# Attention by key-stationary products: split values stationary, split transposed probabilities of two tiles moving, gates transposed instead of results, and a new order of the work around branch C

## What is computed

```python
pr = split_projection(x @ w_in)
o_a = dsa_attention(aq, ak, av, iq, ik, pr['i_w'])      # top-k sparse
o_b = moba_attention(bq, bk, ...)                        # block sparse
o_c = rms_norm(diff_attention(cq, ck, cv, lam), diff_norm) * (1.0 - lam_init)
o_d = mla_attention(qn, qr, kn, kr, dv)
o_e = memory_attention(...)
y = o * jax.nn.silu(z)                                   # z: gates, per branch
u = jnp.einsum('btnc,ncd->btnd', y, w_branch)
out = jnp.sum(jax.nn.sigmoid(g) * u, axis=2) @ w_out
return layer_norm(DN_ALPHA * x + out, ln_g, ln_b)
```

## Time and profile before

| | |
|---|---|
| median of 3 runs | 1382.11 us (1380.39 to 1382.39) |
| the profiled execution | 1384.15 us, of which the span is 1382.5 us |
| PE busy | 1328.0 us, 96% of the span |
| DVE, ACT, POOL busy | 661.8, 653.3, 669.9 us |
| mean granted TensorE clock | 0.985 |
| DMA | 116.47 MB, mean 84 GB/s |

### The profile page before, as it was taken

One profiled execution on the slowest core, in us unless ns is written; L12 is line 12 of the kernel. 1 busy time (PEld: TensorE's weight loads), 2 busy tenths in 40 slices (PEclk: granted clock), 3 DMA queues, 4 the chain that ended last, 5 costly groups with the idle time before them and its releaser, 6 DMA issues.

```text
span 1382.5 us, 19021 instructions
## 1 busy us (share of the span) xinstructions
PE 1328.0 (96%) x6872; PEld 1130.7 (82%) x6872; DVE 661.8 (48%) x1609; ACT 653.3 (47%) x1296; POOL 669.9 (48%) x850
## 2 busy tenths in 40 slices
PE   6999999999988999999999999999999899999995
PEld 5888878888877898888888888888888779888884
DVE  4646696433155753213265668753322665432044
ACT  4455345454275664423245543555434665643232
POOL 3543453255563444467464435334446434645764
PEclk9899999999998999999999999999999999999998
DMA  7322242231331143232413223223123213323221
GB/s 258 114 77 62 81 114 58 67 88 47 103 95 37 37 123 107 58 107 77 140 49 106 68 71 106 81 58 85 53 74 111 59 33 86 95 65 100 84 77 61
DMA packets 147052, 116.47 MB, mean 84 GB/s; under 512 B 5520, under 2 KB 131856, under 8 KB 146704
## 3 DMA queue, kind: packets, MB, share of 16 engines
q1 hardware_dynamic: 146816, 114.22, 27.8%
q10 hardware_dynamic: 144, 1.05, 0.2%
HBM read 112.10 MB, written 3.15 MB: 83 GB/s over the span
## 4 chain that ended last, share of the span: by engine, by line
PE 79%; DVE 12%; ACT 4%; issue 2%; POOL 1%; DMA 1%; SPq 0%; POOLq 0%; DVEq 0%; ACTq 0%
PE product L737 19%; PE product L738 18%; PE product L739 18%; PE context L977 5%; PE scores L949 3%; PE transposed L962 3%; PE branch_product L737 2%; PE branch_product L739 2%; PE branch_product L738 2%; DVE index_scores L1389 2%; DVE top_eight L1395 1%; DMA residual<-in_x_dram 1%; ACT score_operands L1001 1%; POOL residual L677 1%; DVE vector_scratch L1214 1%
## 5 line engine op out<-in xcount | busy, mean ns | idle before, releaser
L721 POOL TENSOR_TENSOR weights_rest<-raw_weights,weights_head 128x320 fp32r<-128x320 f32 (+3 forms) x672 | 540.1, 836 | 376.8 <-ACT weights_head L1001 376.8
L737 PE MATMUL product<-weights_head,stationary_head 128*128 128x512 f32 (+3 forms) x768 | 291.4, 379 | 7.8 <-POOL weights_rest L721 7.6
L1001 ACT ACTIVATE weights_head<-raw_weights 128x1280 fp32r<-128x1280 f32 (+4 forms) x178 | 198.3, 1115 | 200.3 <-PE product L739 153.5
L739 PE MATMUL product<-weights_head,stationary_rest 128*128 128x512 f32 (+3 forms) x768 | 285.6, 372 | 0.0
L738 PE MATMUL product<-weights_rest,stationary_head 128*128 128x512 f32 (+3 forms) x768 | 285.4, 372 | 0.0
L737 PE MATMUL product<-stationary_head,weights_head 128*128 128x512 f32 x640 | 263.5, 412 | 0.0
L738 PE MATMUL product<-stationary_rest,weights_head 128*128 128x512 f32 x640 | 252.6, 395 | 0.0
L739 PE MATMUL product<-stationary_head,weights_rest 128*128 128x512 f32 x640 | 252.1, 394 | 0.0
L704 POOL TENSOR_TENSOR merged<-merged,activated 128x256 f32<-128x256 f32 x128 | 93.0, 748 | 291.4 <-DVE activated L1533 291.2
L737 PEld LDWEIGHTS product<-weights_head,stationary_head 128*128 128x128 f32 x768 | 145.7, 190 | 29.8 <-POOL weights_rest L721 8.4
L739 PEld LDWEIGHTS product<-weights_head,stationary_rest 128*128 128x128 f32 x768 | 145.4, 189 | 23.7
(11 more groups left out here) (200 smaller groups left out, 1812.5 us busy)
## 6 DMA issues: line engine op xcount, KB each, us to landing
raw_weights<-in_w_in_dram SPq DMA_DIRECT2D x104, 512.0 KB, 3.7
raw_weights<-in_w_in_dram SPq DMA_DIRECT2D x72, 256.0 KB, 2.9
raw_weights<-in_w_branch_dram SPq DMA_DIRECT2D x80, 128.0 KB, 3.7
raw_weights<-in_w_out_dram SPq DMA_DIRECT2D x16, 512.0 KB, 3.6
merged<-in_w_mem_kv_dram SPq DMA_DIRECT2D x8, 512.0 KB, 7.3
raw_weights<-in_w_in_dram SPq DMA_DIRECT2D x8, 416.0 KB, 3.1
raw_weights<-in_w_in_dram SPq DMA_DIRECT2D x8, 296.0 KB, 3.8
residual<-in_x_dram SPq DMA_DIRECT2D x4, 512.0 KB, 11.4
```

Of the source, the lines that this page charges most:

```text
L721: ins = nc.gpsimd.tensor_tensor(WL[:, sw, part], RAW[:, sr, part], WH[:, sw, part].bitcast(F32), ALU.subtract)
L737: nc.tensor.matmul(dst, sh, mh, start=start, stop=False)
L739: return nc.tensor.matmul(dst, sl, mh, start=False, stop=stop)
L1001: return nc.scalar.activation(dst, src, ACT.Copy, scale=scale)
```

## The change

In branches A and D (WIDE):

- V is done once for two query tiles. Stationary are 128 keys of [values head, values rest] (`vs`, 128 columns); moving are the transposed probabilities of the tile pair, split in head `ph` and rest `pl`: 256 columns, or 128 where only the later tile sees the keys. All passes are fp32r. The output is the transposed result in two halves of 64 partitions, head and rest.
- The new step pr (DVE) makes `pl`; T's copy by ACT makes `ph`. The bank TP is free for the next T after pr, not after the copy. The new step vs splits a head's values (ACT, then DVE).
- fo is now an ACT copy of one half of the result (64 x 512), and the new step fa (DVE) adds the other half. fin multiplies the gate by the reciprocal row sums. The new step zj transposes the gates on PE into G2 and G3, where DVE multiplies them with the result; yj has no transpose left, and splits what lies in `probabilities_T` and `vector_scratch`.

For branch C, W stands half a step earlier and the pieces of ev and er are laid singly and earlier; the first qt uses the banks U and O, and the attention starts in chunk C1 instead of gA0. In chunk IX the groups go through three units for the first two tiles, in O1 through the units of a tile before the next tile, and l1 and l2 are spread among them. The early split of the next layer's first unit is gone, two splits stand earlier in `start`, and the fourth tile of x is loaded after two units of weights. The diff, cut:

```diff
+WIDE = "AD"
...
+def wide_steps(b):
...
+    if b == "D":
+        out = [[("qt", b, 0)], [("ev", b, 0)], [("er", b, 0), ("qt", b, 1)], [("ev", b, 1)], [("er", b, 1)], [("vs", b, 0)]]
+    else:
+        out = [[("qt", b, 0)], [("ev", b, 0), ("er", b, 0)], [("ev", b, 1), ("er", b, 1)], [("vs", b, 0)]]
+    for i in range(UNITS + LAG_V + 1):
+        first, second = [], []
+        u = i - LAG_V
+        if 0 <= u < UNITS and u % 2 == 1:
+            first.append(("V", b, u))
+        if u >= NT and u % NT == 0:
+            first.append(("fa", b, u // NT - 1))
+        if 0 <= i - LAG_T < UNITS:
+            first.append(("T", b, i - LAG_T))
+            second.append(("pr", b, i - LAG_T))
+        if i < UNITS:
+            second.append(("S", b, i))
+        if i in (4, 8):
+            second += prep_steps(b, 1 + i // 4)
+        if i in (5, 9):
+            first.append(("er", b, 1 + i // 4))
+        if 0 <= u < UNITS and u % NT == NT - 1:
+            j = u // NT
+            second += [("fo", b, j)] + ([("vs", b, j + 1)] if j + 1 < NH else []) + [("fin", b, j)]
+        if i == 12:
+            second.append(("zj", b, 0))
+        if u == UNITS:
+            second.append(("zj", b, 1))
+        out += [first, second]
+    return out
...
-    out = [[("qt", "C", 0)], [("ev", "C", 0, 0)], [("er", "C", 0, 0), ("ev", "C", 0, 1)], [("er", "C", 0, 1)], []]
...
+    out = [[("qt", "C", 0)]] + [[] for _ in range(5)]
+    early = {}
+    for j in range(NH):
+        for n in range(4):
+            m, part = divmod(n, 2)
+            at = {0: n - 5, 1: n}.get(j, 2 * (4 * j - 3) + 1 + n)
+            early.setdefault(at, []).append(("ev", "C", j, m, part))
+            early.setdefault(at + 1, []).insert(0, ("er", "C", j, m, part))
...
     for i in range(UNITS + 3):
-        first, second, third = [], [], []
+        first, second = [], []
         if 0 <= i - 3 < UNITS:
             first.append(("V", "C", i - 3))
+            if (i - 3) % NT == NT - 1:
+                first.append(("fo", "C", (i - 3) // NT))
+                second.append(("fin", "C", (i - 3) // NT))
         if 0 <= i - 2 < UNITS:
             first.append(("T", "C", i - 2))
         if i < UNITS:
             first.append(("S", "C", 2 * i))
-            second.append(("S", "C", 2 * i + 1))
+            second.insert(0, ("S", "C", 2 * i + 1))
         if 0 <= i - 1 < UNITS:
-            second.insert(0, ("W", i - 1))
-        second += late
-        late = []
-        if i >= 3 and (i - 3) % NT == NT - 1:
-            first.insert(1, ("fo", "C", (i - 3) // NT))
-            third.append(("fin", "C", (i - 3) // NT))
+            first.append(("W", i - 1))
         if i == 4:
-            third.append(("qt", "C", 1))
-        j, m = divmod(i + 3, 4)
-        if j < NH and m < 2 and i < UNITS:
-            third.append(("ev", "C", j, m))
-            late = [("er", "C", j, m)]
-        out += [first, second + third]
+            second.append(("qt", "C", 1))
+        out += [first + early.get(2 * i, []), second + early.get(2 * i + 1, [])]
...
-    ("lambda", ("gB1", 3, 3), ("C0", 0, 2), 0.0),
-    ("C attention", ("gA0", 0, 0), ("D0", 3, 2), 0.0),
+    ("lambda", ("gB0", 2, 0), ("gB0", 2, 0), 0.0),
+    ("C attention", ("C1", 0, 2), ("D0", 3, 1), 0.0),
...
+        order = [(u, t) for u in range(units(c)) for t in range(parts(c))]
+        if c == "IX":
+            order = [(u, t) for t in range(2) for u in range(3)] + [(u, t) for u in range(3) for t in (2, 3)] + [(3, t) for t in range(NT)]
+        elif c == "O1":
+            order = [(0, t) for t in range(NT)] + [(1, 0), (1, 1), (2, 0), (3, 0), (2, 1), (3, 1)] + [(u, t) for t in (2, 3) for u in range(1, 4)]
+        groups += [(c, u, t) for u, t in order]
...
-    start = [("ln0", 0), ("ln0", 1), ("mkv", 0), ("ln0", 2), ("xj", 0, 0), ("xj", 0, 1), ("ln0", 3), splits[0], ("mkv", 1),
-             ("xj", 1, 0), ("xj", 1, 1), ("ln0", 4), splits[1], splits[2]]
-    extra[at[(ORDER[0], 1, 0)]] += [("xj", 2, 0), ("xj", 2, 1)]
-    extra[at[(ORDER[0], 1, 1)]] += [("xj", 3, 0), ("xj", 3, 1)]
-    extra[at[(ORDER[0], 2, 0)]].append(("ek",))
+    start = [("ln0", 0), ("ln0", 1), ("mkv", 0), ("ln0", 2), ("xj", 0, 0), ("xj", 0, 1), splits[0], splits[1], ("mkv", 1),
+             ("xj", 1, 0), ("xj", 1, 1), ("ln0", 3), splits[2], ("ln0", 4)]
+    extra[at[(ORDER[0], 1, 1)]] += [("xj", 2, 0), ("xj", 2, 1)]
+    extra[at[(ORDER[0], 2, 1)]] += [("xj", 3, 0), ("xj", 3, 1)]
+    extra[at[(ORDER[0], 3, 1)]].append(("ek",))
...
-    extra[at[("O1", 2, 1)]] += [("ahead",) + WEIGHTS[0]]
-    extra[at[("O1", 3, 1)]] += [("l1", 0)]
-    extra[at[("O1", 3, 2)]] += [("l1", 1), ("l2", 0)]
-    extra[at[("O1", 3, 3)]] += [("l1", 2), ("l2", 1), ("l1", 3), ("l2", 2), ("l2", 3)]
+    for t in range(NT - 1):
+        i, j = {0: (("O1", 2, 1), ("O1", 3, 1))}.get(t, (("O1", 1, t + 1), ("O1", 2, t + 1)))
+        extra[at[i]].append(("l1", t))
+        extra[at[j]].append(("l2", t))
+    extra[at[("O1", 3, 3)]] += [("l1", 3), ("l2", 3)]
...
             if b == "C":
-                return G[2], G[3], HD * (j % 2)
+                (_, qs), (_, ks) = qt_banks(b, j // 2)
+                return qs, ks, HD * (j % 2)
...
+            if b == "D":
+                ph, pl = KLZ[:].rearrange("p a n -> p (a n)"), PL[:]
+            else:
+                ph, pl = (TL[:, a:a + 2, :].rearrange("p a n -> p (a n)") for a in (4, 6))
+            return [x.rearrange("p (i n) -> p i n", i=NT) for x in (ph, pl)] + [TL[:, 8, :].rearrange("p (i c d) -> p i c d", i=NT, c=2)]
...
+        def y_rows(k):
+            return PT if k == 0 else DS
...
-            load_x(3)
...
                 for i, item in enumerate(LOADS):
+                    if L == 0 and i == 2:
+                        load_x(3)
...
+                    elif kind == "zj":
+                        _, b, k = step
+                        claim(f"G{2 + k}")
+                        pe.wait_ge(final.sem, final.at(L, (b, 2 * k + 1)))
+                        for t in range(NT):
+                            last = nc.tensor.transpose(G[2 + k][:, t * P:(t + 1) * P],
+                                                       VZ[:, vz(b), t, BW + k * P:BW + (k + 1) * P], ident)
+                        last.then_inc(t_done.sem, t_done.step(step))
+                        freed[f"G{2 + k}"] = (gated, L, step)
...
+                        freed["TP"] = (rest, L, ("pr", b, u)) if b in WIDE else (moved, L, step)
+                    elif kind == "V" and step[1] in WIDE:
+                        _, b, u = step
+                        j, t = divmod(u, NT)
+                        ph, pl, vs = wide(b)
+                        if t == 1:
+                            claim("O")
+                            pe.wait_ge(rest.sem, rest.at(L, ("vs", b, j)))
+                        pe.wait_ge(rest.sem, rest.at(L, ("pr", b, u)))
+                        blocks = [(0, ph), (t, ph), (t, pl)] + [(i, p) for i in range(1, t) for p in (ph, pl)]
+                        blocks.insert(3 if t == 1 else 1, (0, pl))
+                        for n, (i, p) in enumerate(blocks):
+                            at = P if i == t else 0
+                            last = nc.tensor.matmul(O[:, (t - 1) * P + at:(t + 1) * P], vs[:, i].rearrange("p c d -> p (c d)"),
+                                                    p[:, i, at:2 * P], start=n == 0, stop=n == len(blocks) - 1)
+                        last.then_inc(v_done.sem, v_done.step((b, u)))
+                        if t == NT - 1:
+                            freed["O"] = (summed, L, (b, j))
...
+                    elif kind == "vs":
...
+                        _, b, j = step
+                        if j > 0:
+                            act.wait_ge(v_done.sem, v_done.at(L, (b, NT * j - 1)))
+                        else:
+                            act.wait_ge(copied.sem, copied.at(L, ("dk" if b == "D" else b + "1", NT - 1)))
+                        copy(wide(b)[2][:, :, j % 2, :], VZ[:, vz(b), :, j * HD:(j + 1) * HD]).then_inc(moved.sem, moved.step(step))
+                    elif kind == "fo" and step[1] in WIDE:
+                        _, b, j = step
+                        r, o = rows(j)
+                        act.wait_ge(v_done.sem, v_done.at(L, (b, NT * j + NT - 1)))
+                        copy(y_rows(j // 2)[r, :], O[o, :]).then_inc(moved.sem, moved.step(step))
...
+                        if b in WIDE:
+                            half = slice(t % 2 * P, (t % 2 + 1) * P)
+                            copy(wide(b)[0][:, 0:t + 1, half], TP[:, 0:w].rearrange("p (i n) -> p i n", n=P)).then_inc(moved.sem, moved.step(step))
...
+                    elif kind == "pr":
+                        _, b, u = step
+                        t, _, w = unit(b, u)
+                        ph, pl, _ = wide(b)
+                        half = slice(t % 2 * P, (t % 2 + 1) * P)
+                        dve.wait_ge(moved.sem, moved.at(L, ("T", b, u)))
```

(16 more changed lines are left out.)

129 lines of the change are left out of this document (76 added, 53 removed).

## The result

The changed kernel takes 1400.77 us (median of 4 runs, 1398.52 to 1401.18), the kernel before beside it 1381.25 us (4 runs, 1379.29 to 1382.39): ratio 1.014, 95% interval 1.0122 to 1.0157. It is **slower by 19.5 us**; 1355.8 us was predicted, with 1372 as the upper end. The span of its profiled execution is 1399.3 us against 1382.5.

What follows compares the result with a forecast made beforehand. PE was taken to bound the kernel, busy 1328.0 of 1382.5 us. Terms 1 to 5, -10.8 - 22 + 13 - 1 - 5.5 = -26.3 us, gave a median of 1355.8 us (chance 0.50), range 1340 to 1372.

Steps and rivals of the forecast that it cites:

- Term 4: Starts of the layers: first groups' 4.1 us wait goes, a like one comes at the third; -1 us, bounds -7 and +4.
- Term 3: Ends of heads in A and D: V waits for pr in DVE's queue; +13 us, bounds 0 and 26.
- Term 1: V in A and D: fewer, wider passes, 1.33 us a head instead of 2.0; -10.8 us, bounds -7 and -15.
- Term 2: Branch C: waits for W and er go, and their clock loss; -22 us, bounds -12 and -25.
- W's half: Branch C: W a half step earlier, two half steps ahead of T instead of one, fits with 2 us to spare.
- late next would be ACT: Branch C: sixteen copies for the first two heads fall in chunk C1 beside ACT's own activations; 3 us left for it.
- Rival B: Branch C keeps half of its waits, ACT or DVE being late: 12 us gained instead of 22, 1365.8 us; chance 0.12.
- Term 5: The tail: POOL has one tile left, 4 pieces, and the last transfers go earlier; -5.5 us, bounds -3 and -8.
- D: Rival: slower, 12 ends of heads wait 2 us each with a 2 us clock fall behind each; 1390.8 us; chance 0.04.
- rival C: Ends of heads: the SBUF port shared by DVE and POOL stretches vs and fin by 8 us; 1363.8 us; chance 0.08.

Runs made afterwards that it cites:

- e1: The changed kernel with the memory keys' split (ek) put back ahead of the fourth group of chunk IX: 1388.89 us, 11.9 us less than the changed kernel.
- e10: The changed kernel with the third weights' split of IX earlier and the load of tile 3 of x behind those weights' load: 1393.97 us, 6.8 us less.
- e2: The changed kernel with the whole start of a layer (IX's group order, ek, x loads, early split) as in the kernel before: 1380.03 us, 20.7 us less.
- e3: The changed kernel with the wide form off, A and D in the form before: 1388.28 us, 12.5 us less.
- e4: The changed kernel with branch C's plan, banks and eviction as in the kernel before: 1410.82 us, 10.0 us more; it doesn't compute the whole program.
- e7: The changed kernel with C's evictions (ev and er) of heads 2 and 3 one half step earlier: 1392.42 us, 8.4 us less.
- e5: e2 and e3 together, so that of the change only C and the tail are left: 1367.73 us, ratio 0.9911 to the kernel before.
- e8: e5 with e7's edit: 1363.99 us, ratio 0.9877 to the kernel before, 3.7 us below e5.
- e9: e8 with the wide form of A and D put back and their heads' closing step (reciprocals, fin) one tile later: 1365.21 us, ratio 0.9879 to before.
- e11: The changed kernel with the edits of e1, e7 and e10, and the heads' closing step in A and D one tile later: 1362.24 us, ratio 0.9850 to before.
- e12: e11 with branch A alone in the form before: 1361.29 us, ratio 0.9849 to the kernel before.

## Why the prediction was wrong

**Term 4, starts of the layers: -1 predicted, +18.6 measured, and the step that turned the sign.** Two things failed. The first is an omission: the working of the term has ln0, xj and the splits, and not ek, which the diff moves from behind (IX,2,0) to behind (IX,3,1). No one asked who waits for it (bank U, wanted by the index transposes) and what it is moved past on its engine (two tiles of index rotations). e1 shows 11.9 us for that alone. The second is "I find PE waiting there about as long": 4.1 us were carried over from a wait with another queue behind it, and it was 8.9. The prediction saw that the third split stood behind ln0 of the last tile, and then took the old wait's size instead of adding up the queue on ACT and POOL. e10 gives 6.8 us. Together 18.7 of the 20.7 us that e2 takes off.

**Term 3, waits at the ends of heads: +13 predicted, 16.4 measured.** The mechanism and the places were right: the three of A were given as 1.3, 2.0 and 0.5 and were 1.11, 2.08 and 1.16; those of D as 1.1, 0.4 and 1.1 and were 0.87, 0.43 and 1.13. Two kinds were left out: the last V of D (0.80) and small ones on V inside a head (0.27 to 0.37). And the clock: two falls in A cost 1.6 us each (A costs 5.5 us a layer with them, 3.9 in e2's trace, where there are none).

**Term 1, V: -10.8 predicted.** A head's V takes 1.52 us in the mean (1.56 in A, 1.48 in D), not 1.33, so the saving is 0.49 us a head, 7.8 us. The pitch of 0.12 was right inside a run of passes; the passes around them, at the start of a step and at each change of width, take more: the term is mis-sized, within its bound of -7. V, waits and falls give -7.8 + 16.4 + 3.2 = 11.8 us, beside 12.5 by e3 and 14.6 in the table. The rest stood in no term: in e2's trace the product passes of A and D, the same in number, take 1.0 us a layer more than before, and the transposes of D's keys 0.4.

**Term 2, C: -22 predicted, -11.3 measured** (10.0 by e4). W's half was right, its wait is gone. The step that failed is "the last er before a head's first scores ends a half step earlier". It doesn't: the plan puts it into half step 8j - 1, behind the mask of that same step, and the old one stood there too; only its neighbour was moved away. The four waits measure 6.7 us against 6.1. e7 moves them that half step, which is worth 2.3 us a layer. The rest is a new wait for the row maxima in chunk C1 (406.88 and 1089.76, 2.1 us each) with a fall of the clock behind each, 1.6 us more. In layer 0:

```profile
403.52 1.19 ACT L1088 ACTIVATE score_operands<-branch_product 32x512 fp32r<-32x512 f32 x2
...
405.50 0.97 DVE L1667 SCALAR_TENSOR_TENSOR values_and_gates<-activated,product 128x256 f32<-128x256 f32 x2 [1.06 <-ACT values_and_gates L1088]
...
406.88 0.45 PE L1017 MATMUL scores<-score_operands 96*128 96x384 f32 x1 [2.08 <-DVE negated_maxima L1562]
```

The chunk's own work on ACT stands behind the copies for branch C, DVE waits for it, and the mask stands behind DVE's part: "late next would be ACT" was right, and 3 us for both layers too little. Rival B, half of the waits kept, was the true case of this branch.

**Term 5, the tail: -5.5 predicted, -5.5 measured** behind the last product pass. POOL's last run is the four pieces forecast:

```profile
1391.02 3.75 POOL L735 TENSOR_TENSOR residual<-residual,values_and_gates 128x256 f32<-128x256 f32 x4 [1.95 <-DVE residual L1351]
...
1394.29 1.68 DVE L1403 SCALAR_TENSOR_TENSOR residual<-residual,norm_stats,values_and_gates 128x512 f32<-128x512 f32 x2
1395.34 1.09 SPq L722 DMA_DIRECT2D out_dram<-residual  x2
```

The last transfers now wait for DVE, not for POOL, and the span ends 12.0 us behind the start of the last product pass (1387.34), where it was 17.5 (1365.03).

**The sum.** Predicted -26.3, measured +16.8 in the traces, 43 us apart: 20 from term 4, 12 from terms 1 and 3, 11 from term 2. No rival was the case. D had slower waits at the ends as its cause, but e3, in which they are all gone, is still 7 us slower than before. Of the falls of the clock that D expected behind each end two came, both in A, at 1.6 us each. What D lacked was the starts, to which no rival was given, and the far end of term 4's bounds, +4, stood only on the wait that was seen.

The port (rival C) can be in it with 2.4 us, not with the 8 of that rival; no run kept POOL off these operations. At eight of the twelve ends vs and fin measured 0.42 and 0.43 us, as at the end shown above. At the third end of A they took

```profile
341.05 1.09 DVE L1427 TENSOR_TENSOR score_operands<-values_and_gates,score_operands 128x256 fp32r<-128x256 f32 x1 [1.70 <-ACT score_operands L1088]
...
342.46 0.70 DVE L1460 TENSOR_TENSOR values_and_gates<-values_and_gates,reciprocals 128x256 f32<-128x256 f32 x1
```

while POOL ran (340.14 to 343.34), and V there waited 1.16 us where 0.5 was forecast; the third end of D has a vs of 0.67, and layer 1 is the same. The prediction took its 0.42 from L1421 as a mean over both cases. It isn't one: that operation has one input in PSUM, and all 40 of it took 0.42.

## What to carry to other kernels

Go through every line of a diff that moves a step, also the one that looks like a detail, and ask three things of it: which bank or buffer it frees, who wants that next, and what it now stands behind on its engine. A wait whose queue changes is to be summed anew from that queue; its old length is no estimate. And where a plan is given in half steps, print both plans and compare the place of the last step that someone waits for: here one line of a moved formula left it where it was.

## What the runs showed that was not expected

- The clock takes or returns some 1.6 to 1.7 us at a time, and not by the waits alone. In C's first head five traces (e5, e8, e9, e11, e12) have the same wait of 2.1 us on the row maxima, at 389 to 391 us; passes at the low level follow it in e8 and e12 and not in the three others. In A, a fall follows V's wait of 2.08 us in the changed kernel, and in e7, whose waits there are the same, none does. So an edit's worth depends on its base: e7's gave 8.4 us on one and 3.7 on the other. What decides is open; each kernel was traced once.
- In spite of that the four edits of e11 add up: 38.7 us one by one, 38.5 together.
- An operation of DVE on 128 x 36 elements with two inputs in SBUF (L1322, in the rotations that ek stood behind) took 0.89 us at 59.63, while POOL ran (51.79 to 60.74), and 0.19 us at 62.49 in e1's trace, where POOL stood idle. It is what rows 9 showed, here in a queue that PE waited for. The Trainium skill, "SBUF — State Buffer", section "SBUF: two separate sides", states such a lock between the two engines, and these traces agree with it; no run here kept POOL off them, so what it adds to ek's 11.9 us wasn't measured.
